# Expert stage of a decoder step: down bias summed once, gate/up bias on four row groups, new tokens' scatter in eight products

## What is computed

```python
logits = tok @ w_router + b_router
top_val, top_idx = lax.top_k(logits, TOP_K)          # 4 of 32 experts for each of 288 tokens
top_w = jax.nn.softmax(top_val, axis=-1)
...
    gu = xe @ w_gate_up[e] + b_gate_up[e]            # 1024 -> 2048
    g = jnp.minimum(gu[:, 0::2], SWIGLU_LIMIT)
    u = jnp.clip(gu[:, 1::2], -SWIGLU_LIMIT, SWIGLU_LIMIT)
    act = (u + 1.0) * (g * jax.nn.sigmoid(SWIGLU_ALPHA * g))
    return act @ w_down[e] + b_down[e]               # 1024 -> 1024
...
out = jnp.zeros((n_tok, d)).at[row_tok].add(yb * row_w[:, None])
```

## Time and profile before

| | |
|---|---|
| median of 3 runs | 1505.27 us |
| profiled execution, its span | 1499.6 us |
| PE busy | 1416.6 us, 94% of the span |
| DVE, ACT, POOL busy | 28%, 19%, 2% of the span |
| chain of work that ended last | PE 90%, DVE 5%, ACT 4%, issue 1% |
| DMA | 470.19 MB, mean 314 GB/s |

### The profile page before, as it was taken

The page is one execution under the profiler, slowest core; times in us unless marked ns, Lnnn a source line. Parts: engine busy times, 40 slices in busy tenths (PEclk is TensorE's granted clock), DMA queues, the critical chain, the costliest instruction groups (busy, mean ns, idle before and its releaser), DMA issues.

```text
span 1499.6 us, 16322 instructions
## 1 busy us (share of the span) xinstructions
PE 1416.6 (94%) x6562; PEld 542.2 (36%) x6562; DVE 414.1 (28%) x663; ACT 279.0 (19%) x519; POOL 34.2 (2%) x42
## 2 busy tenths in 40 slices
PE   7997788997788999999999999999999999999998
PEld 3476444344442333333333333333333333333332
DVE  1347720134042222223222222222222222222223
ACT  2135233113321111111111111111111111111110
POOL 0012400000000000000000000000000000000000
PEclk9998778998987999999999999999999999999999
DMA  9151078742183999999999999999999999999992
GB/s 346 72 194 39 1 259 338 255 174 90 56 336 143 368 382 394 377 394 397 399 389 385 400 399 401 391 387 397 397 401 400 381 395 390 382 395 384 382 390 85
DMA packets 95533, 470.19 MB, mean 314 GB/s; under 512 B 6401, under 2 KB 6657, under 8 KB 60660
## 3 DMA queue, kind: packets, MB, share of 16 engines
q1 hardware_dynamic: 93812, 463.69, 78.8%
q0 software_dynamic: 1696, 6.14, 1.3%
HBM read 463.94 MB, written 5.88 MB: 313 GB/s over the span
## 4 chain that ended last, share of the span: by engine, by line
PE 90%; DVE 5%; ACT 4%; issue 1%; DMA 0%; SPq 0%; DVEq 0%; ACTq 0%
PE PS L907 30%; PE PS L943 16%; PE PS L887 7%; PE PS L869 6%; PE PS L837 4%; PE PS L363 4%; PE PS L663 3%; PE PS L390 2%; PE PS L917 2%; PE PS L705 2%; PE PS L878 1%; PE PS L623 1%; PE PS L932 1%; PE PS L952 1%; PE PS L717 1%; ACT arena L1681 1%
## 5 line engine op out<-in xcount | busy, mean ns | idle before, releaser
L907 PE MATMUL PS<-ring,arena 128*64 128x512 f32 x1792 | 410.7, 600 | 0.8 <-ACT arena L1779 0.8
L1463 DVE TENSOR_TENSOR X<-X,PS 128x1024 f32<-128x1024 f32 (+1 forms) x99 | 120.3, 1217 | 695.9 <-PE PS L887 695.9
L943 PE MATMUL PS<-ring,arena 128*64 128x512 f32 x1024 | 241.6, 615 | 0.0
L907 PEld LDWEIGHTS PS<-ring,arena 128*64 128x64 f32 x1792 | 120.6, 137 | 276.1 <-issue 276.1
L1791 ACT ACTIVATE arena<-arena 128x512 f32<-128x512 f32 x32 | 20.1, 629 | 553.9 <-DVE arena L1484 553.9
L943 PEld LDWEIGHTS PS<-ring,arena 128*64 128x64 f32 x1024 | 69.7, 140 | 147.4 <-issue 120.9
L887 PE MATMUL PS<-arena 64*128 64x512 f32 x396 | 111.2, 640 | 0.9 <-ACT arena L1799 0.9
L869 PE MATMUL PS<-arena 128*64 128x512 f32 (+1 forms) x396 | 98.1, 613 | 2.9 <-issue 2.9
L837 PE MATMUL PS<-arena 32*64 32x512 f32 x264 | 71.3, 618 | 0.0
L887 PEld LDWEIGHTS PS<-arena 64*128 64x128 f32 x396 | 30.0, 184 | 80.6 <-issue 80.6
L907 PE MATMUL PS<-arena 128*64 128x512 f32 x256 | 57.6, 592 | 0.0
(11 more groups left out here) (323 smaller groups left out, 1083.4 us busy)
## 6 DMA issues: line engine op xcount, KB each, us to landing
ring<-in_w_gate_up SPq DMA_DIRECT2D x112, 2048.0 KB, 11.8
ring<-in_w_down SPq DMA_DIRECT2D x64, 2048.0 KB, 10.0
arena<-in_w_gate_up SPq DMA_DIRECT2D x16, 2048.0 KB, 15.0
ring<-in_w_in SPq DMA_DIRECT2D x6, 2048.0 KB, 17.2
ring<-in_cache_win_k SPq DMA_DIRECT2D x8, 1024.0 KB, 7.1
ring<-in_cache_win_v SPq DMA_DIRECT2D x8, 1024.0 KB, 10.8
ring<-in_w_out SPq DMA_DIRECT2D x2, 2048.0 KB, 13.8
ring<-in_cache_mem_k SPq DMA_DIRECT2D x4, 1024.0 KB, 7.7
```

The costliest lines, as they stand in the source:

```text
L907: last = mm(PS[64 * half:64 * half + 64, nb, :], XT[:, k, :], w[:, k % 2, c:c + 512], start=False, stop=k == KT - 1, tile_position=(0, 64 ...
L943: last = mm(PS[64 * half:64 * half + 64, 5, :], AT[:, k % 4, 64 * (k // 4):64 * (k // 4) + 64], w[:, k % 4, half * 512:(half + 1) * 512], ...
L1463: v.tensor_tensor(x, x, PS[0:n, b:b + 2, :], ALU.add).then_inc(sem("scatter_added"), 1)
```

## The change

1. **Down bias.** The two products of L917 and the table `BD` go. The down products start their sum themselves (`start=k == 0`). In exchange the first scatter, which carried zeros, carries the biases: POOL loads the two halves of `b_down` into rows 0 to 31 and 64 to 95 of `YB` once DVE has cleared it, DVE copies the routing weights of all 32 experts to `SELW`, PE turns them, and ACT puts them into `SW`. So each token gets the weighted sum of its experts' down biases once.
2. **Gate/up bias.** `BGU` holds four quarters of 512 columns on the four groups of 32 partitions, loaded by four DMAs; `EROW` has 128 rows. The four products of an expert's bias stand together behind the gather, on tiles (0, 0), (64, 64), (32, 0) and (96, 64), and none is left between the transposes and the down products.
3. **New tokens' scatter.** Instead of two products of 64 rows by 128 columns by 512, eight of 64 rows by 32 columns by 128, on eight tiles. The new tokens' residual stands in `XS4`, four column blocks on four groups of 32 partitions, so that DVE adds 256 columns instead of 1024. ACT fills `XS4` ahead of the loop, and SP stores it at the end with four DMAs instead of one. PE's wait for DVE's second add stands ahead of k = 5 instead of behind it.
4. The turn of the routing weights is numbered one on, since there is one more, ahead of the loop.

```diff
-        BGU = ar(5376, 2 * FF)
-        BD = ar(7424, D)
+        BGU = ar(5376, 512)
...
+        XS4 = ar(5888, 2, P)
...
-            def gate_up_biases(n, nb):
+            def gate_up_biases(n):
                 pe.wait_ge(sem("erow_ready"), n + 1)
-                for half in range(2):
-                    c = half * 1024 + nb * 512
-                    mm(PS[64 * half:64 * half + 64, nb, :], EROW[0:NE, :], BGU[0:NE, c:c + 512],
-                       start=True, stop=False, tile_position=(0, 64 * half))
-            pe.wait_ge(sem("expert_biases_loaded"), 32)
-            gate_up_biases(0, 0)
-            gate_up_biases(0, 1)
+                for nb, half in halves:
+                    r = 32 * (2 * half + nb)
+                    mm(PS[64 * half:64 * half + 64, nb, :], EROW[r:r + 32, :], BGU[r:r + 32, :],
+                       start=True, stop=False, tile_position=(r, 64 * half))
+            pe.wait_ge(sem("expert_biases_loaded"), 96)
+            gate_up_biases(0)
...
+            def turn_weights(n):
+                pe.wait_ge(sem("selw_ready"), n + 1)
+                for t in range(3):
+                    m = ROWS[t]
+                    last = nc.tensor.transpose(PS[:, 3, COL0[t]:COL0[t] + m],
+                                               SELW[0:m, t].rearrange("p a s -> p (a s)"), ident[0:m, 0:m])
+                last.then_inc(sem("sw_turned"), 1)
+            turn_weights(0)
...
-                if banks == (6, 7):
+                if banks == (6, 7) and t < 2:
                     pe.wait_ge(sem("scatter_added"), n + 1)
                 for half in range(2):
                     r = slice(64 * half, 64 * half + 64)
-                    last = mm(PS[:, banks[half], :], SW[r, t * P:(t + 1) * P], YB[r, :],
-                              start=True, stop=True)
+                    if t < 2:
+                        last = mm(PS[:, banks[half], :], SW[r, t * P:(t + 1) * P], YB[r, :],
+                                  start=True, stop=True)
+                        continue
+                    for c in range(4):
+                        last = mm(PS[32 * c:32 * c + 32, banks[half], 0:P], SW[r, SEQ:NTOK],
+                                  YB[r, c * P:(c + 1) * P], start=True, stop=True,
+                                  tile_position=(64 * half, 32 * c))
...
+                    if k == 5:
+                        pe.wait_ge(sem("scatter_added"), 3 * q + 3)
...
-                        for half in range(2):
-                            mm(PS[64 * half:64 * half + 64, 5, :], EROW[0:NE, :],
-                               BD[0:NE, half * 512:(half + 1) * 512],
-                               start=True, stop=False, tile_position=(0, 64 * half))
                         scatter(3 * q, 0)
...
-                gate_up_biases(it + 1, 0)
+                gate_up_biases(it + 1)
                 pe.wait_ge(sem("act_ready"), it + 2)
...
-                gate_up_biases(it + 1, 1)
...
-                                  start=False, stop=k == KT - 1, tile_position=(0, 64 * half))
+                                  start=k == 0, stop=k == KT - 1, tile_position=(0, 64 * half))
...
+            v.tensor_copy(SELW[:, :, :, 0:NE], bc(GW[:, 0:NE, :].rearrange("p e t -> p t e"), 2, 2)
+                          ).then_inc(sem("selw_ready"), 1)
...
+                if t < 2:
+                    x, y = X[:, t, :].rearrange("p (b c) -> p b c", b=2), PS[:, b:b + 2, :]
+                else:
+                    x, y = XS4, PS[:, b:b + 2, 0:P]
+                v.tensor_tensor(x, x, y, ALU.add).then_inc(sem("scatter_added"), 1)
...
+            for c in range(4):
+                pool.dma_start(BGU[32 * c:32 * c + 32], bgu[:, c * 512:(c + 1) * 512]
+                               ).then_inc(sem("expert_biases_loaded"), 16)
+            pool.wait_ge(sem("y_rows_ready"), 1)
+            bd = a["b_down"].rearrange("l e f -> (l e) f")
+            for half in range(2):
+                pool.dma_start(YB[64 * half:64 * half + NE], bd[:, half * 512:(half + 1) * 512]
+                               ).then_inc(sem("expert_biases_loaded"), 16)
```

More of the change, by code:

```diff
@@ L944, in expert @@
                                   w[:, k % 4, half * 512:(half + 1) * 512],
-                                  start=False, stop=k == KT - 1, tile_position=(0, 64 * half))
+                                  start=k == 0, stop=k == KT - 1, tile_position=(0, 64 * half))
                     if k == 3:
                         last.then_inc(sem("expert_units_used"), 1)
[L949 to L954, removed]
+                        turn_weights(it + 1)
                         turn_gathered(q + 1)
@@ L1392, in expert_row @@
             def expert_row(e):
-                v.tensor_scalar(EROW[0:NE, :], cst("ones")[0:NE, 0:SLOTS], cst("expert")[0:NE, bass.ds(e, 1)], None,
+                v.tensor_scalar(EROW, cst("ones")[:, 0:SLOTS], cst("expert")[:, bass.ds(e, 1)], None,
                                 ALU.mult).then_inc(sem("erow_ready"), 1)
@@ L1400, in _ @@
             v.memset(YB, 0.0).then_inc(sem("y_rows_ready"), 1)
-            v.memset(SW[:, 0:P], 0.0).then_inc(sem("sw_ready"), 1)
-            v.memset(SW[:, P:3 * P], 0.0).then_inc(sem("sw_cleared"), 1)
+            v.memset(SW[:, NTOK:3 * P], 0.0).then_inc(sem("sw_cleared"), 1)
+            step(v.memset(SELW, 0.0))
             v.memset(AC, 0.0).then_inc(sem("act_ready"), 1)
@@ L1459, in add_scattered @@
             def add_scattered(t, b):
-                n = ROWS[t]
-                x = X[0:n, t, :].rearrange("p (b c) -> p b c", b=2)
-                v.tensor_tensor(x, x, PS[0:n, b:b + 2, :], ALU.add).then_inc(sem("scatter_added"), 1)
+                if t < 2:
[3 more added lines that the diff above has]
+                v.tensor_tensor(x, x, y, ALU.add).then_inc(sem("scatter_added"), 1)
+            dve.wait_ge(sem("sw_ready"), 1)
             dve.wait_ge(sem("npass_ready"), 1)
@@ L1506, in _ @@
                 dve.wait_ge(sem("scatter_added"), last + 4)
+                dve.wait_ge(sem("sw_ready"), r * NE + NE + 1)
                 v.memset(SW, 0.0).then_inc(sem("sw_cleared"), 1)
@@ L1766, in _ @@
                 square_rows(X, t)
+            for c in range(4):
+                s.copy(XS4[32 * c:32 * c + 32],
+                             X[0:NTS, 2, :].rearrange("p (h c k) -> p h c k", h=2, c=4)[:, :, c, :])
             act.wait_ge(sem("logits_ready"), 1)
@@ L1780, in keep_columns, with keep_weights @@
                        PS[:, 2, :].rearrange("p (c h s) -> p c h s", c=4, h=2)).then_inc(sem("xt_ready"), 1)
+            def keep_weights(n):
+                act.wait_ge(sem("sw_turned"), n + 1)
+                s.copy(SW[:, 0:NTOK], PS[:, 3, 0:NTOK]).then_inc(sem("sw_ready"), 1)
+            keep_weights(0)
             act.wait_ge(sem("npass_ready"), 1)
@@ L1794, in _ @@
                     s.copy(AT, PS[:, 4, :].rearrange("p (c n) -> p c n", c=4)).then_inc(sem("at_ready"), 1)
-                    act.wait_ge(sem("sw_turned"), it + 1)
-                    s.copy(SW[:, 0:NTOK], PS[:, 3, 0:NTOK]).then_inc(sem("sw_ready"), 1)
+                    keep_weights(it + 1)
                     keep_columns(q + 1)
@@ L1892, in _ @@
             pool.wait_ge(sem("mem_stored"), 32)
[L1893 to L1896, removed]
+            bgu = a["b_gate_up"].rearrange("l e f -> (l e) f")
+            for c in range(4):
+                pool.dma_start(BGU[32 * c:32 * c + 32], bgu[:, c * 512:(c + 1) * 512]
[5 more added lines that the diff above has]
+                               ).then_inc(sem("expert_biases_loaded"), 16)
             pool.wait_ge(sem("prompt_state_stored"), 16)
@@ L2036, in _ @@
             for t in range(3):
-                n = ROWS[t]
-                dst = o["y_prompt"][0, t * P:(t + 1) * P] if t < 2 else o["y_sample"].rearrange("b t d -> (b t) d")
                 sp.wait_ge(sem("scatter_added"), npass * (3 * (NE + 1)) + max(t - 1, 0))
-                sp.dma_start(dst, X[0:n, t, :]).then_inc(sem("rows_stored"), 16)
-            sp.wait_ge(sem("rows_stored"), 48)
+                if t < 2:
+                    sp.dma_start(o["y_prompt"][0, t * P:(t + 1) * P], X[:, t, :]).then_inc(sem("rows_stored"), 16)
+                    continue
+                for c in range(4):
+                    dst = o["y_sample"].rearrange("b t (h c k) -> c (b t) h k", h=2, c=4)[c]
+                    sp.dma_start(dst, XS4[32 * c:32 * c + 32]).then_inc(sem("rows_stored"), 16)
+            sp.wait_ge(sem("rows_stored"), 16 * 6)
             sp.wait_ge(sem("prompt_state_stored"), 16)
```

1 line of the change is left out of this document (added).

## The result

The changed kernel takes 1435.18 us, the median of four runs (1433.38 to 1439.41), against 1505.09 beside it: a ratio of 0.9537, with an interval of 0.9521 to 0.9553. Forecast were 1442 us and a range of 1434 to 1473. The gain is 69.9 us where the sum had 63.1; some 5 us of the difference are the clock's.

A forecast was written before the change was run, and what follows sets the result against it. PE's instruction stream in the expert loop was taken as the bound. Savings of 1.88 us an expert, 60.2 for 32, and 3.4 of clock, less 0.5 for the start, brought 1505.3 to 1442 us, range 1434 to 1473.

The forecast's parts named there:

- Down bias: Expert loop, PE's chain: the down bias products go and nothing comes back, saving 1.00 us an expert.
- Gate/up bias: Expert loop: four products side by side take 0.86 us; PE then waits 0.7 us for ACT, saving 0.27 us, not 1.00.
- New tokens' scatter: Expert loop: eight small products take 0.45 to 0.69 us instead of 1.06; 0.45 taken, saving 0.61 us an expert.
- later than 1.32 us: Expert loop, sign of a wrong forecast: down products begin later than 1.32 us after the transposes.
- Clock: Expert loop: five falls of 1.68 us become three, 3.4 us gained; ends were none (8.4 gained) or every expert (45 lost).
- The moved wait: Ahead of k = 5, PE waits for the second scatter's add; 0.5 us is left over, so it costs nothing.
- Start: Ahead of the loop: PE's first gate/up bias waits for the down table's load, between 0 and 4 us once; 0.5 taken.
- End: After the loop: DVE's shorter last add and four stores at about 0.4 us an issue cancel, 0 plus or minus 1 us.
- Transfers: Expert loop loads: 29.6 us an expert at 425 GB/s against PE's 29.95, so they do not set the time yet.
- the 13 us in hand: Expert loop: a down load lands at the latest at 922.1 and is used at 935.77 at the earliest, over 13 us.
- The second rival: Expert loop: transfers become the bound, an expert staying at up to 32.1 us, 1450 to 1505 us in all; chance 0.06.
- The 5.7 us above the span: Whole run: the median of the runs stood 5.7 us above the profiled execution's 1499.6 us span; the difference was carried over.

The follow-up runs named there:

- the three kernels that take back one part each: Changed kernel with down bias per expert back, 1469.41 us; gate/up bias pairs on one row group around the transposes, 1463.97; new tokens' scatter as two wide products, 1457.12.
- the two with 30.89 and 30.57 us: Changed kernel with the down bias back in every expert, 1469.41 us; changed kernel with the new tokens' scatter as two wide products, 1457.12 us.
- the three kernels that wait for transfers: Changed kernel with prompt scatters cut to 64 columns, 1431.03 us; routing weights turned behind the activation's transposes, 1430.0; that turn plus a separate down-bias wait, 1427.7.
- The last experiment: Changed kernel with routing weights turned behind the activation's transposes, plus a semaphore of its own for the down bias table: 1427.7 us, ratio 0.9464.
- the cut scatters: Changed kernel with the prompt tokens' two scatters cut from 512 to 64 columns of each half, loads unchanged: 1431.03 us in a single run, ratio 0.950.

## Why the prediction was right, and where its terms were off

**Down bias: right.** 1.00 us predicted and measured, from both sides.

**Gate/up bias: right to 0.01 us.** The four products take 0.85 (0.86 predicted), and the gain is not the pair's 1.00 but 0.27, since ACT's copy is on the chain now (0.59 us an expert, where I wrote "0.3 us or so"). The timeline that answers to the earlier trace rows:

```profile
909.27 0.66 PE L945 MATMUL PS<-CN,arena 128*128 128x128 f32 x4
909.97 0.58 ACT L1816 COPY arena<-PS 128x512 f32<-128x512 f32 x1 [0.84 <-PE PS L945]
910.60 1.94 PE L955 MATMUL PS<-ring,arena 128*64 128x512 f32 x8 [0.67 <-ACT arena L1816]
```

From the transposes to the down products are 1.33 us, 1.32 predicted; of PE's idle time, 0.67 us against 0.7. I had called "later than 1.32 us" a sign of being wrong, which left no room for the last digit.

**New tokens' scatter: mechanism right, 0.07 us too dear.** 0.38 instead of 0.45; the bounds for the price were 0.45 to 0.69, so it fell below the lower one. The term that was mis-sized is the sum of two rounds at 0.12 us and 0.20 us for the change of shape, which I took from the wide products. The trace shows that the eight tiles run side by side: the first eight records begin 7 ns apart, from 931.62 to 931.67, the second eight from 931.76, and the next group at 932.00. If the rounds take 0.12 us each, 0.14 is left for the change of shape; how the 0.38 splits is not shown. The Trainium skill, page "TensorEngine Tiling (Array Packing)", section "Instruction Overhead", gives each matmul an overhead of some 60 cycles, which paid by 16 records one after another is an estimate of 0.40 us for the products alone; the trace has 0.38 for products and change of shape together, so here the records overlap. The sum per expert is 1.95 us instead of 1.88, and the three kernels that take back one part each (1.00, 0.26, 0.68) add up to it within 0.01; times 31 it is 60.4 us. With 8.4 us of clock that gives the 68.8 between the traces.

**Clock: the larger miss, 5 us.** I took three falls and got none, an end of my bounds. Over nearly the whole loop the stretches' table shows the clock at 1.00:

```profile
560.00:1420.00 860.00, 840.43 (x4348) 271.72 (x4346) 205.16 (x318) 133.96 (x201) 0.00 (x0) 1.00 1.01 414
```

The failed step is where I weighed the fuller stretch against 0.7 us of idle time and split the difference. The experiments tell more. Idle time ahead of down doesn't bring the falls: the changed kernel and the two with 30.89 and 30.57 us have it in every expert and have no fall. They come back in the two kernels whose bias stands on one group of 32 rows (ten and four falls; five before the change). Why the pairs around the transposes bring ten, and the same pairs ahead of them four, all at the end, stays open; idle time may even have spared some. Since the ten come in every third expert and the four in a row, where an expert stands in time seems to matter too, so the counts are no price of a pair. That the bias on four row groups ends the falls is the reading that fits all of them; whether the groups themselves do it, or the shorter stretch (0.85 us of bias products instead of 1.72 or 1.86), is not separated, and the three kernels that wait for transfers have no place in this count.

**The moved wait: right, nothing.** Waits by waiter and releaser show (us, times, mean us)

```profile
PEld PS L925 <- DVE X L1475: 10.8, 32, 0.3
```

so weight loads wait 0.3 us there, where I had read 0.5 us left over: they come ahead of their products. PE itself does not wait: in the chain k = 5 follows without a gap, and with the wait behind k = 5 again the period differs by the scatter's 0.68 alone.

**Start: 1.07 instead of 0.5 us.** The chain there, and DVE's mask from the timeline:

```profile
445.85 0.46 POOL arena L1921
446.34 5.69 DMA arena<-in_b_down
452.07 1.99 PE PS L838 x8
454.06 2.02 PE PS L851 x12
```

```profile
452.07 0.81 DVE L1440 TENSOR_REDUCE arena<-arena 128x96 f32<-128x384 f32 x1
453.99 2.08 PE L851 MATMUL PS<-arena,CN 128*128 128x32 f32 x12
```

The down table lands 5.7 us after issue, not the 3.4 and "a little more" that I charged; I had said that the prefetch beside it could add some. PE starts the bias at 452.07 and the next products at 453.99, 1.07 us behind the mask (452.88 plus 0.04). The last experiment takes just this away. That the net cost still came out at 0.5 is luck: the first expert should end 1.95 us earlier for its savings, and it ends 1.4 earlier by the marks above. Half of the delay came back because the clock rises 27 us behind the clearing of `YB` in both traces, so that the later first gate and up group has less of the low clock, 5.36 us instead of 5.88.

**End: 1.1 us longer, just past my "0, plus or minus 1".** DVE's add shrank as expected (421 ns), but SP takes 0.8 us for each of the four stores, where I put 0.4:

```profile
1432.49 3.25 SPq L2069 DMA_DIRECT2D out_y_sample<-arena  x4
```

**Transfers: right that they don't set the time yet, wrong on the reason.** I took 29.6 us an expert, from 425 GB/s in one stretch of 4 us. Sustained it is 418 GB/s and 30.1 us, so PE at 29.89 is already faster than its loads. What saves it is the other half of the argument, the 13 us in hand. The trace shows that being used up: issue to landing on the ring (least, median, most) at 500 to 580 us, and at 1330 to 1415.

```profile
DMA to landing us min/median/max: 10.9/14.2/16.4
```

```profile
DMA to landing us min/median/max: 17.9/20.1/22.3
```

The median grows by 6 us in 28 experts, as 0.2 us each would make it. The second rival therefore was much nearer than its chance suggests: by an estimate from these numbers, with another 0.3 us off PE's chain the 13 us would be gone after 26 experts, and the loads would bind, as they do in the last three kernels. The Trainium skill, page "DMA: Bandwidth & Descriptors", section "Specifications", names two limits, about 358 GB/s of HBM for a core and 435 for the fabric; the stretch behind the cut scatters holds 418 for some 700 us, above the first and below the second.

**The 5.7 us above the span: a wrong reading.** I carried them over as time around the span. In all four runs of the changed kernel that time is 1.9 to 2.0 us; the rest was scatter, since with 2.0 us around its span the profiled execution before took an estimated 1501.6, less than any of the runs beside it. The sum of the change's terms didn't rest on it.

## What to carry to other kernels

Small-row products (a bias by a one-hot row, a scatter to few tokens) belong side by side on all row and column groups: here four products of 32 rows cost what two do, and with them the falls of the clock were gone, which was worth as much as the instructions saved there (8.4 us, against 32 times 0.27). Which property of the products ended them is open. Before a product is counted as gained, look at what it covered: here 1.00 us of bias hid an ACT copy and brought 0.27. And price the next bound by its sustained rate, from a run in which it binds, and count the lead separately: a loop can run faster than its loads for as long as the lead lasts.

## What the runs showed of the hardware that I had not expected

- Sixteen records of 64 rows by 32 columns by 128 on eight tiles take 0.38 us, with the change of tile shape within it, and eight of them begin within 0.05 us; two products of 64 rows by 128 by 512 take 1.06.
- The granted clock fell from 0.99 to 0.51 behind PE work without a gap, in kernels with the bias pairs on one row group, and stayed at 1.00 with 0.67 us of idle time in every expert of the changed kernel.
- Two POOL-issued loads of 64 KB landed after 5.2 and 5.7 us in the changed kernel, one of 128 KB, issued at another place, after 3.4 in the kernel before.
- A store of 32 partitions in four column blocks keeps SP for 0.8 us each, while the undivided one took 0.56.
